# Moving the delta branch's convolution units from beside the attention to beside the second projection's first part

## The reference, cut to what matters

```
def _dn_prepare(qkv_raw, b_raw, a_raw, w, pos):
    qkv = jax.nn.silu(_short_conv(qkv_raw, w['conv_w']))
    q, k, v = jnp.split(qkv, [DN_QK_W, 2 * DN_QK_W], axis=-1)
    q = _l2norm(_heads(q, DN_HEADS))
    k = _l2norm(_heads(k, DN_HEADS))
    v = _heads(v, DN_HEADS)
    if pos is not None:
        q = _rope_2d(q, pos[0], pos[1])
        k = _rope_2d(k, pos[0], pos[1])
    q = q * DN_DK ** -0.5
```

## Time and profile before

| | us |
|---|---|
| median of 3 runs (3939.7 to 3945.2) | 3941.4 |
| profiled execution | 3946.9 |
| its span from first to last instruction | 3945.1 |
| PE busy | 3242.1 (82%) |
| DVE busy | 2131.0 (54%) |
| ACT busy | 1318.4 (33%) |
| POOL busy | 572.8 (15%) |
| mean granted clock of PE | 0.888 of 2.4 GHz |

### The profile page before, as it was taken

The page is one execution under the profiler, slowest core; times in us unless marked ns, Lnnn a source line. Parts: engine busy times, 40 slices in busy tenths (PEclk is TensorE's granted clock), DMA queues, the critical chain, the costliest instruction groups (busy, mean ns, idle before and its releaser), DMA issues. The chain is left out here.

```text
span 3945.1 us, 82620 instructions
## 1 busy us (share of the span) xinstructions
PE 3242.1 (82%) x36108; PEld 2686.1 (68%) x36108; DVE 2131.0 (54%) x3567; ACT 1318.4 (33%) x2374; POOL 572.8 (15%) x466
## 2 busy tenths in 40 slices
PE   7999977758799999445497998888888688887599
PEld 7988864544598888434345998877777577776244
DVE  3455538868424555589574110667777444544453
ACT  3133325634312333356233110344444222221441
POOL 0200004521011000355010000011111122221100
PEclk9999986768899999656698999988999799999799
DMA  4522222234335121231333222634332311111430
GB/s 136 171 92 69 78 65 66 82 103 128 118 118 167 63 76 47 62 71 36 134 123 120 87 84 90 211 130 134 119 121 94 114 44 47 47 39 26 170 114 32
DMA packets 270356, 377.43 MB, mean 96 GB/s; under 512 B 46373, under 2 KB 209501, under 8 KB 268776
## 3 DMA queue, kind: packets, MB, share of 16 engines
q1 hardware_dynamic: 167930, 259.18, 21.3%
q10 hardware_dynamic: 102066, 112.97, 8.3%
HBM read 255.10 MB, written 118.94 MB: 95 GB/s over the span
## 5 line engine op out<-in xcount | busy, mean ns | idle before, releaser
L366 PE MATMUL psum<-proj_w_low,h_high 128*128 128x344 f32 (+1 forms) x1984 | 662.8, 334 | 0.0
L366 PE MATMUL psum<-proj_w_high,h_low 128*128 128x344 f32 (+1 forms) x1984 | 654.8, 330 | 0.0
L366 PE MATMUL psum<-proj_w_high,h_high 128*128 128x344 f32 (+1 forms) x1984 | 653.7, 329 | 0.0
L366 PEld LDWEIGHTS psum<-proj_w_low,h_high 128*128 128x128 f32 x1984 | 374.7, 189 | 10.4 <-issue 4.5
L366 PEld LDWEIGHTS psum<-proj_w_high,h_high 128*128 128x128 f32 x1984 | 375.1, 189 | 6.5
L366 PEld LDWEIGHTS psum<-proj_w_high,h_low 128*128 128x128 f32 x1984 | 374.4, 189 | 4.4
L389 DVE COPY proj_y<-psum 128x344 f32<-128x344 f32 (+1 forms) x130 | 70.5, 542 | 427.1 <-PE psum L366 427.1
L366 PE MATMUL psum<-proj_rest_w_low,h_high 128*128 128x304 f32 x640 | 215.1, 336 | 28.4 <-DVE proj_rest_w_low L378 22.1
L1358 PE MATMUL psum<-w_out,merge_yt 128*128 128x512 f32 x512 | 227.3, 603 | 1.8 <-DVE merge_yt L1241 1.8
L802 POOL TENSOR_TENSOR scan_d<-scan_b 128x384 f32<-128x384 f32 x112 | 123.6, 1103 | 622.0 <-DVE scan_b L643 609.0
L412 ACT ACTIVATE proj_y<-psum 128x344 f32<-128x344 f32 (+1 forms) x130 | 62.3, 479 | 451.2 <-PE psum L366 438.0
(11 more groups left out here) (384 smaller groups left out, 6963.6 us busy)
## 6 DMA issues: line engine op xcount, KB each, us to landing
proj_raw<-in_w_in SPq DMA_DIRECT2D x24, 1376.0 KB, 7.1
proj<-proj_y ACTq DMA_DIRECT2D x192, 172.0 KB, 1.9
dn_prep_x<-proj SPq DMA_DIRECT2D x90, 256.0 KB, 3.5
delta_x<-dn_qkv SPq DMA_DIRECT2D x40, 384.0 KB, 5.1
proj<-proj_y ACTq DMA_DIRECT2D x68, 224.0 KB, 1.9
proj_raw<-in_w_in SPq DMA_DIRECT2D x7, 1792.0 KB, 8.0
modulate_w<-in_mod_w SPq DMA_DIRECT2D x16, 768.0 KB, 4.7
merge_z<-proj SPq DMA_DIRECT2D x8, 1536.0 KB
```

The costliest lines, as they stand in the source:

```text
L366: last = PE.matmul(self.ps[:, j % self.banks, 0:self.width], hp[:, kt, tokens], wp[:, c % 2, kt, :], start=kt == 0 and n == 0, stop=kt == ...
```

## The change

The units move from the second call to the first: `DeltaPrepareLate` stands beside the norm and the projection with start 22 and step 0.37, and the attention's call has four stages left. The units are ordered part by part (all ten tiles of q, then k, then v) in place of tile by tile. There are three sets of buffers in place of two, and all waits for unit u - 2 become waits for unit u - 3. The projection takes its column groups in the order 2, 3, 4, 5, 0, 1, 6, so that the convolution's columns come first, and SP waits, before a unit's loads, for the last four stores that the unit's tile and its neighbours need (`projected`). The buffers of the units lie where the norm's lay, so SP waits for the norm's last transposes before the first load. The waits for the convolution's weights get a place in the order (`yield -3`) in place of standing at the very front.

```diff
 class DeltaPrepare(Stage):
+    SETS = 3
+    def __init__(self, k, name, units, p2, dn, bottom=None):
...
-        self.units = [(tile, part) for tile in tiles for part in range(3)]
+        self.units = units
...
     def sp_unit(self, u):
...
-        if u >= 2:
-            SP.wait_ge(*self.conv(u - 2))
+        if u >= self.SETS:
+            SP.wait_ge(*self.conv(u - self.SETS))
+        self.projected(u)
         for d in range(3):
             SP.dma_start(self.x[:, s, d], self.p2[r + d - 1:r + d - 1 + P, c0:c0 + C]).then_inc(*loaded.inc())
...
     def dve(self):
+        yield -3
         self.nc.vector.wait_ge(*self.consts(0))
         yield from self.each(self.dve_unit)
...
 class DeltaPrepareLate(DeltaPrepare):
+    def sp(self):
+        if self.norm is not None:
+            yield -6
+            self.nc.sync.wait_ge(*self.norm.transposed(self.norm.n - 1))
+        yield from super().sp()
+
+    def projected(self, u):
+        if self.project is not None:
+            tile, part = self.units[u]
+            last = self.project.first[part + 1] + min(tile + 1, NT2 - 1)
+            for j in range(last - 3, last + 1):
+                self.nc.sync.wait_ge(*self.project.kept[j % 4](j // 4))
...
     def pool_unit(self, u):
...
-        if u >= 2:
-            G.wait_ge(*self.done(u - 2))
+        if u >= self.SETS:
+            G.wait_ge(*self.done(u - self.SETS))
...
-        project = Project(k, "proj2", norm.top, h, [range(NT2)] * 6 + [late], w2, 448, p2, row_of=row2, normed=norm, ctx=h_ctx)
+        project = Project(k, "proj2", above + 57344, h, [range(NT2)] * 6 + [late], w2, 448, p2, row_of=row2, normed=norm, ctx=h_ctx, order=(2, 3, 4, 5, 0, 1, 6))
+        early = DeltaPrepareLate(k, "dn_prep", [(tile, part) for part in range(3) for tile in range(NT2)], p2, dn, above, norm=norm, project=project)
...
-        together(k, (norm, 0, 1.0), (project, 1, 1.0))
+        together(k, (norm, 0, 1.0), (project, 1, 1.0), (early, 22, 0.37))
...
-        prepare = DeltaPrepareLate(k, "dn_prep", range(NT2), p2, dn, gates.top)
...
-        together(k, (rest, 1, 1.0), (gates, 4, 1.5), (na, 1, 0.6), (prepare, 20, 0.5), (attention, 23, 0.9))
+        together(k, (rest, 1, 1.0), (gates, 4, 1.5), (na, 1, 0.6), (attention, 23, 0.9))
```

More of the change, by code:

```diff
@@ L1884 @@
     CONVOLVED = 1.6
-    def __init__(self, k, name, tiles, p2, dn, bottom=None):
+    SETS = 3
+    def __init__(self, k, name, units, p2, dn, bottom=None):
         super().__init__(k, name, bottom)
+        Z = self.SETS
         self.p2, self.dn = p2, dn
         t, sig, C = self.tile, self.event, self.C
-        self.units = [(tile, part) for tile in tiles for part in range(3)]
+        self.units = units
         n = len(self.units)
-        self.x, self.w = t("x", [P, 2, 3, C]), t("w", [P, 3, 3 * C])
-        self.y, self.e, self.tmp = t("y", [P, 2, C]), t("e", [P, 2, C]), t("tmp", [P, 2, C])
-        self.ss, self.rs, self.rp = t("ss", [P, 2, 8]), t("rs", [P, 2, 8]), t("rp", [P, 2, 64])
+        self.x, self.w = t("x", [P, Z, 3, C]), t("w", [P, 3, 3 * C])
+        self.y, self.e, self.tmp = t("y", [P, Z, C]), t("e", [P, Z, C]), t("tmp", [P, Z, C])
+        self.ss, self.rs, self.rp = t("ss", [P, Z, 8]), t("rs", [P, Z, 8]), t("rp", [P, Z, 64])
         loads, stores = [3 + self.turns(u) for u in range(n)], [1 if tile >= NCTX else 2 for tile, _ in self.units]
         self.consts = sig("dma", "consts", 1)
[L1897 to L1900, removed]
+        self.loaded = [sig("dma", f"loaded{s}", sum(loads[s::Z])) for s in range(Z)]
+        self.stored = [sig("dma", f"stored{s}", sum(stores[s::Z])) for s in range(Z)]
+        self.loads = [sum(loads[u % Z:u + 1:Z]) - 1 for u in range(n)]
+        self.stores = [sum(stores[u % Z:u + 1:Z]) - 1 for u in range(n)]
         self.conv, self.logs = (sig("dve", x, n) for x in ("conv", "logs"))
@@ L1918, in sp_unit @@
     def sp_unit(self, u):
[L1919 removed]
+        SP, s, (tile, part), C = self.nc.sync, u % self.SETS, self.units[u], self.C
         loaded, r, c0 = self.loaded[s], row2(tile), CONV + C * part
         yield -5.5
[L1922 to L1923 removed]
+        if u >= self.SETS:
+            SP.wait_ge(*self.conv(u - self.SETS))
+        self.projected(u)
         for d in range(3):
@@ L1949, in dve_unit @@
     def dve_unit(self, u):
-        V, c, s, (_, part) = self.nc.vector, self.k.vo.chain, u % 2, self.units[u]
+        V, c, s, (_, part) = self.nc.vector, self.k.vo.chain, u % self.SETS, self.units[u]
         y, e, tmp, ss, rs = self.y[:, s], self.e[:, s], self.tmp[:, s], self.ss[:, s], self.rs[:, s]
@@ L1953, in dve_unit @@
         V.wait_ge(*self.loaded[s](self.loads[u]))
-        if u >= 2:
-            V.wait_ge(*self.stored[s](self.stores[u - 2]))
+        if u >= self.SETS:
+            V.wait_ge(*self.stored[s](self.stores[u - self.SETS]))
         yield from self.convolve(u, y, tmp)
@@ L1989, in act @@
     def act(self):
+        yield -3
         self.nc.scalar.wait_ge(*self.consts(0))
         yield from self.each(self.act_unit)
-        for s in range(2):
+        for s in range(self.SETS):
             self.nc.scalar.wait_ge(*self.stored[s](self.stored[s].total - 1))
     def act_unit(self, u):
-        S, c, s, (tile, part) = self.nc.scalar, self.k.so.chain, u % 2, self.units[u]
+        S, c, s, (tile, part) = self.nc.scalar, self.k.so.chain, u % self.SETS, self.units[u]
         y, e, rs = self.y[:, s], self.e[:, s], self.rs[:, s]
```

19 lines of the change are left out of this document (12 added, 7 removed).

## The result

The changed kernel takes 3919.8 us in the median of four runs (3912.0 to 3925.8), beside 3943.3 us for the kernel before (four runs); the ratio is 0.9937 with an interval of 0.9914 to 0.9960. The change makes the kernel 0.63% faster, where I forecast 3950 and no difference that can be told. The profiled execution took 3912.0 us (span 3910.2) and is the fastest of the four.

What follows compares the result with a forecast made beforehand. PE alone bounds the first stage; in the attention DVE's in-order queue makes PE wait. Cost +94 less gain 85 is +9 on the profiled 3946.9, so 3955.9, less 5.5 to the runs' median: 3950 us, range 3900 to 3990.

Steps and rivals of the forecast that it cites:

- The onset of the second stage: Start of the second stage: 6 us gained without the convolution's weight load, 6 us without the first unit ahead of the attention.
- Rival C: First stage keeps PE's pace, DVE's work filling 226 us almost exactly: +15 - 85 gives 3871 us; chance 0.05.
- rival A: POOL's first taps keep out of DVE's way and the attention stage reaches its floor: 63 - 100 gives 3904; chance 0.22.
- The cost, +94: First stage: it follows DVE, which carries the moved units, and ends later by 94 us, bounds 60 and 115.
- The gain, 85: Second stage: 73 us from the attention's steps plus 6 and 6 at the onset, bounds 60 and 108.
- what stays late once the convolution is gone: Attention stage: lateness remaining after the units leave, 42 us in all, giving 436 us and a gain of 73.
- the floor: Attention stage: 32 undisturbed pairs of steps at 12.3 us, 394 us against 509 now.
- gaps without a half item: Attention stage: some 12 of 128 gaps have nothing to cover ScalarE's copy or the exponential, 0.8 us each, 10 us.
- the 14 weight splits: Attention stage: seven splits on each of DVE and ACT, about 1.3 us each past the slack, 18 us.
- three changes of head pair: Attention stage: values, bias table and POOL addition have to come anew, 3 us each, 9 us.
- low clock: Attention stage: lower PE clock after the remaining late spots, 5 us.
- B: Attention stage: the chain from transposes to exponential takes over, only 43 us gained: 94 - 43 gives 3992; chance 0.23.

Runs made afterwards that it cites:

- doubled maximum: Changed kernel with the maximum over the scores done twice in each of the 64 attention steps: 3932.6 us, ratio 0.9951 to the kernel before.
- small splits: Changed kernel with the rest projection's last seven weight splits cut to 19 of 304 columns, DVE's only (3917.2 us) or DVE's and ACT's (3912.0 us).
- the split: Changed kernel with 20 q and k units beside the first stage (all taps on DVE, start 16), 10 v units beside the attention (POOL's taps): 3863.9 us.
- low parts made twice: Changed kernel with the rest projection's last seven weight splits on DVE done a second time into unread memory: 3948.8 us, ratio 0.9992.

## Why the prediction was right or wrong

**What was right.** The reading of the kernel before held: DVE's in-order queue made PE late in the attention, and the change takes that away. The first stage follows DVE. Of the signs named beforehand, DVE is busy 80% of the stretch (over 75%) at a clock of 0.91, PE waits 51.5 us from 2226 to 2530 (over 40; 32.5 of them name L389), the last addition waits for POOL in all 30 units and takes 1.62 us in the mean (1.6; some 1.7 in 28 of them). One reading was off: PE idles 43 of the 226 us, a fifth and not a third. The onset of the second stage came out at -12.7 for 12. Rival C and the first half of rival A are ruled out by the same numbers: POOL's taps do not keep out of DVE's way.

**The cost, +94 for 83.9.** The row of units took 10.48 us a unit instead of 10.7, and their end, DVE's last operation of the last unit (L1969 at 2530.0, 0.7 us long), lies 13 us before my 2544. The first stage itself began 2 us earlier in this execution. The 286 us of unit work were nearly right: most units of the values took 7.9 to 8.4 us (8.0 in the working), the context units 9.6 to 10.0 (9.5), most others 10.5 to 11.1 (10.5). What was too large is the padding on top of them (26 for the projection's work on DVE, 8 for delays by ACT). A likely reason, not shown by a run of its own, is that part of the projection's copies falls into DVE's waits: 41 us for POOL, 29 for ACT. The wait for the last unit's store came as forecast: that store is issued at 2531.6, ACT's last copy starts at 2534.0.

**The gain, 85 for 110: this is the step that failed**, in the paragraph on what leaves the attention stage, the term "what stays late once the convolution is gone". I put 42 us over the floor. Measured are 19 (413 us from 2649 to 3062, beside 394). Term by term, by the waits of PE after:

| term | charged | measured |
|---|---|---|
| gaps without a half item, ACT's copy or the exponential | 10 | 10.8 (9.8 + 1.0) |
| the 14 weight splits | 18 | some 2 (0 to 5) |
| three changes of head pair | 9 | 4.0 (values by DMA) |
| low clock | 5 | 0 to 5 |

The first term and the floor were right. In the changed kernel the transposes at 2706.94 and 2719.20 bound a pair with seven key blocks and three half items, 12.26 us with one wait of 0.74 us for ACT's copy: 11.52 without it, where the working's rows give 13.24 - 1.76 = 11.48. There are 113 half items in the 63 steps between the transposes, 3.59 a pair (3.62 in the working). Each split was charged with 1.3 us past a slack that the working names but derives from no row: half of DVE's 2.7 us was taken to get through. The doubled maximum shows that most steps have a microsecond to spare, and the runs with small splits show that 2.7 us on DVE and 2.2 on ACT cost next to nothing as they lie, while seven blocks of 5.4 us on DVE cost 17 us of the stage: the lateness does not grow in proportion to the block, as the charge had it. With the 18 at 2 and the 9 at 4, 21 us would have stayed instead of 42, the gain would have been 106, and the forecast 3946.9 - 5.5 + 94 - 106, 3929 us. The bound of 108, which let 20 us stay over the floor, was set to hold such a case and is just passed by the 110 measured.

**What the gain consists of.** I had 77 us of idle time and 38 of low clock over the floor, and let 37 and 5 of them stay: a gain of 40 and 33. Measured are 59.0 and 36.6. The clock's part was right within 4 us, and the miss is in the idle time, as the table of terms says.

**The rivals.** B is ruled out: 17 of the 76 us of idle time stayed, not more than 50, and the doubled maximum gives the chain a microsecond to spare. Rival A carried the right size for the attention stage, 100 us, but tied it to POOL's taps staying out of DVE's way in the first stage. Nothing connects the two, and a rival of its own, 94 - 100, would have stood at 3935. The time lies in the range, 3900 to 3990 (which takes in A, while B's 3992 lies just outside it); the forecast's own range (3925 to 3970) just misses it, and a chance of 0.37 for faster was too low.

## What to carry to other kernels

Before moving work, divide its length on the in-order engine by the room in the new place, and move only what fits: 20 of 30 units fitted without lengthening the stage, where all 30 with the same taps and start lengthened it by 32 us. Look also at how the moved work runs in its new place: with all taps on DVE and the earlier start, the whole move gives 2.1% instead of 0.6%, and the split only a little more, 2.3%. When an engine sets the pace, a helper that makes it wait and lengthens its instructions is no help, and should be taken out. When estimating what stays after a disturbance is gone, look for undisturbed stretches in the trace and charge only what they show, not each possible lateness by its length.

## What the runs showed of the hardware

The exclusion of POOL and DVE is almost a full instruction: an addition of 0.69 us with two SBUF inputs takes 1.62 us beside a multiplication of 1.29 us on POOL that began 0.15 us earlier, and 0.72 us beside one over an eighth of the columns. I had expected it from a single case in the earlier trace rows; that it occurs in nearly every unit once both engines are coupled by the same semaphores (28 of 30), and with two sets of buffers mostly moves to another instruction (24 of 30 units still meet it), was new to me.

Idle time of PE went with lost clock in the runs that disturb this stage. With the low parts made twice PE was idle 29.1 us between the first and the last transposes and busy 394.9; with all taps on DVE idle 14.7 and busy 386.0 with the same matmuls. So 14 us more of idle time came with 9 us of lower granted clock (0.98 against 1.00), and in the run with the doubled maximum 12 us with 13 (0.97). In the kernel before 61 us more of idle time came with 41. Over these differences of 12 us and more, an idle microsecond on PE went with 1.6 to 2 us of length in this stage. It is no fixed price: between the undisturbed profiles it does not hold, for without any units PE was idle 19.3 us and busy 387.2, in the changed kernel idle 17.2 and busy 390.2.
